# Hybrid decoder step: the first mixer group's next weights split ahead of its decay exponents, and the first head's attention steps at later places of the second group

## What is computed

```
proj = x @ w_in                               # 8 sections of 512: hq hf hv hg, rq rk rv rg
f    = lb + (1-lb)*sigmoid(hf);  log_f = log(max(f, 1e-6));  k = (1-lb)*sigmoid(-hf)
o_hg = HGRN2(silu(hq), k, hv, log_f)          # 4 heads of 128: decayed scores, running state
o_hg = rms_norm(o_hg) * g * silu(hg)
o_rt = retention(rotary(rq), rotary(rk), rv)  # 4 heads of 128
o_rt = (group_norm(o_rt)*g + b) * silu(rg)
x    = layer_norm(alpha*x + concat(o_hg, o_rt) @ w_o)
x    = layer_norm(alpha*x + conv_ffn(x))
```

## Time and profile before

| | |
|---|---|
| median of 3 timed runs | 1771.18 us |
| lowest and highest | 1766.13 and 1771.87 us |
| span of the profiled execution | 1765.4 us |
| own time of the profiled execution | not listed apart from its span |
| PE busy (matmul) | 1585.4 us, 90% of the span |
| DVE busy | 930.3 us, 53% |
| ACT busy | 657.9 us, 37% |
| POOL busy | 154.2 us, 9% |

### The profile page before, as it was taken

One profiled execution on the slowest core, in us unless ns is written; L12 is line 12 of the kernel. 1 busy time (PEld: TensorE's weight loads), 2 busy tenths in 40 slices (PEclk: granted clock), 3 DMA queues, 4 the chain that ended last, 5 costly groups with the idle time before them and its releaser, 6 DMA issues.

```text
span 1765.4 us, 31743 instructions
## 1 busy us (share of the span) xinstructions
PE 1585.4 (90%) x12187; PEld 1263.6 (72%) x12187; DVE 930.3 (53%) x1493; ACT 657.9 (37%) x936; POOL 154.2 (9%) x126
## 2 busy tenths in 40 slices
PE   4699999998879999999957999999896999999994
PEld 3577777776658888878745777777674888887883
DVE  5766744443575555533266767444366555553334
ACT  3635423232263433422154544233235443333223
POOL 3111110000020000000030111100002000000002
PEclk8789889998989999999978989999987999999997
DMA  5121231220312233223321222222121323322321
GB/s 185 51 62 51 73 109 62 84 73 26 96 50 94 95 95 95 73 79 90 97 66 48 73 73 73 76 85 73 50 74 47 96 95 95 95 80 71 98 65 51
DMA packets 175036, 137.86 MB, mean 78 GB/s; under 512 B 5064, under 2 KB 169192, under 8 KB 174776
## 3 DMA queue, kind: packets, MB, share of 16 engines
q1 hardware_dynamic: 168192, 113.46, 21.1%
q0 software_dynamic: 5408, 18.60, 3.1%
q10 hardware_dynamic: 1372, 4.95, 0.8%
HBM read 124.91 MB, written 12.07 MB: 78 GB/s over the span
## 4 chain that ended last, share of the span: by engine, by line
PE 76%; DVE 10%; ACT 6%; issue 4%; DVEq 3%; ACTq 1%; DMA 1%; SPq 0%
PE ACC L506 60%; PE SCR L619 2%; PE SCR L536 2%; PE OT L627 2%; ACT WH L825 1%; PE SCR L657 1%; DVE X L1189 1%; PE OT L679 1%; DVE Z L1220 1%; PE OT L595 1%; DVE Fb L1202 1%; DVE WL L1149 1%; DVEq L1259 1%; PE SCR L722 1%; PE OT L594 1%
## 5 line engine op out<-in xcount | busy, mean ns | idle before, releaser
L506 PE MATMUL ACC<-XH,WH 128*128 128x280 f16 x2432 | 503.7, 290 | 74.7 <-DVE XL L1192 43.1
L506 PE MATMUL ACC<-XL,WH 128*128 128x280 f16 x2432 | 502.6, 289 | 0.0
L506 PE MATMUL ACC<-XH,WL 128*128 128x280 f16 x2432 | 502.2, 289 | 0.0
L506 PEld LDWEIGHTS ACC<-XH,WH 128*128 128x128 f16 x2432 | 237.4, 101 | 158.7 <-DVE XL L1192 45.9
L1149 DVE SCALAR_TENSOR_TENSOR WL<-stage,WH 128x2048 f16<-128x2048 f32 (+1 forms) x116 | 245.9, 2120 | 180.8 <-ACT WH L825 169.1
L506 PEld LDWEIGHTS ACC<-XL,WH 128*128 128x128 f16 x2432 | 243.4, 100 | 58.8
L506 PEld LDWEIGHTS ACC<-XH,WL 128*128 128x128 f16 x2432 | 243.5, 100 | 58.4
L825 ACT ACTIVATE WH<-stage 128x2048 f16<-128x2048 f32 (+1 forms) x116 | 204.8, 1765 | 103.0 <-PE ACC L506 85.7
L506 PE MATMUL ACC<-shared,WH 128*128 128x280 f16 x1408 | 225.4, 283 | 0.2
L506 PEld LDWEIGHTS ACC<-shared,WH 128*128 128x128 f16 x1408 | 137.6, 98 | 30.7 <-issue 0.8
L506 PE MATMUL ACC<-shared,WL 128*128 128x280 f16 x704 | 141.3, 283 | 0.0
(11 more groups left out here) (241 smaller groups left out, 1870.7 us busy)
## 6 DMA issues: line engine op xcount, KB each, us to landing
stage<-in_w_in_dram SPq DMA_DIRECT2D x64, 512.0 KB, 4.8
stage<-in_w_a_dram SPq DMA_DIRECT2D x44, 512.0 KB, 4.2
stage<-in_w_b_dram SPq DMA_DIRECT2D x44, 512.0 KB, 4.6
stage<-in_w_down_dram SPq DMA_DIRECT2D x32, 384.0 KB, 3.1
stage<-in_w_down_dram SPq DMA_DIRECT2D x32, 320.0 KB, 3.4
out_dram<-shared POOLq DMA_DIRECT2D x16, 512.0 KB, 3.4
stage<-in_w_o_dram SPq DMA_DIRECT2D x16, 512.0 KB, 3.9
shared<-in_state_hgrn_dram POOLq DMA_DIRECT2D x8, 512.0 KB, 5.8
```

The costliest lines, as they stand in the source:

```text
L506: last = mm(ACC[:, acc, h, 0:HALF], lhs, x[:, xk + k, h * HALF:(h + 1) * HALF], start=begin, stop=end)
```

## The change

In group 0 of each layer, ACT writes the high part of the next unit of half 0 ahead of the read of q and of `hg_exponentials`, and DVE its low part ahead of `hg_exponents`; both stood behind them. Group 1 is taken out of the loop on PE and on DVE, and the loop now runs over groups 2 and 3. In group 1 DVE makes the low part of half 1 ahead of `hg_scores`, and PE places all attention steps of the first head by a new table: scores, transposes and state steps seven slots later, the sample steps, outputs and mean squares three slots later. No instruction is added to or taken from the computation.

```diff
@@ PE
                 group(l, 0)
-                with pe.Fori(0, HEADS - 1) as p:
+                group(l, 1, hg_steps(l, 0, scr_hg(l, 0), HG_SLOTS_FIRST))
+                with pe.Fori(1, HEADS - 1) as p:
                     group(l, p + 1, hg_steps(l, p, scr_hg(l, p), HG_SLOTS))
@@ ACT, group
                 if b is not None:
                     b()
+                if a is None:
+                    split_hi(0, j + 1, (acc_full, 1 + tile + 2))
                 if kind == 0:
                     if d is None:
                         read_acc(Q, 1, tile + 1, None)
                     hg_exponentials(l, head)
                     if d is not None:
                         read_acc(Q, 1, tile + 1, None)
-                split_hi(0, j + 1, (acc_full, 1 + tile + 2))
+                if a is not None:
+                    split_hi(0, j + 1, (acc_full, 1 + tile + 2))
                 if kind == 0:
                     hg_query(l, head)
@@ DVE, hg_query
-            def hg_query(l, p, j, mixed, steps):
+            def hg_query(l, p, j, mixed, steps, split_done=False):
...
-                split_lo(0, j)
+                if not split_done:
+                    split_lo(0, j)
@@ DVE, group
-            def group(l, g, head, kind, stages=(None,) * 4, mixed=None, after_hgrn=False):
+            def group(l, g, head, kind, stages=(None,) * 4, mixed=None, after_hgrn=False, split_first=False):
...
-                if a is not None:
+                if a is not None and not split_first:
                     a()
                 split_lo(1, j)
+                if split_first:
+                    a()
                 if kind == 0:
                     hg_gate(l, head, tile)
+                    if a is None:
+                        split_lo(0, j + 1)
                     hg_exponents(l, head)
...
-                    hg_query(l, head, j + 1, mixed, steps)
+                    hg_query(l, head, j + 1, mixed, steps, a is None)
@@ DVE, layer
                 group(l, 0, 0, 0)
-                with dve.Fori(0, HEADS - 1) as p:
+                group(l, 1, 1, 0, hg_stages(l, 0), ot0 + 2, split_first=True)
+                with dve.Fori(1, HEADS - 1) as p:
                     group(l, p + 1, p + 1, 0, hg_stages(l, p), ot0 + 2 + p)
@@ places
 HG_SLOTS = ([1, 2, 3, 4, 5, 6, 7], [7, 8, 9, 10], [12, 13], [22, 22], [23, 23, 24, 24, 25, 25], [28, 28])
+HG_SLOTS_FIRST = ([8, 9, 10, 11, 12, 13, 14], [14, 15, 16, 17], [19, 20], [25, 25], [26, 26, 27, 27, 28, 28], [31, 31])
```

## The result

The changed kernel takes 1784.39 us, the median of four runs (1781.68 to 1785.97). The kernel before, run beside it, takes 1770.2 us. The ratio is 1.0086, with a 95% interval from 1.0068 to 1.0104: slower, by 14 to 15 us, and outside the 0.3% that count as no change. The forecast was 1784.4 us. The profiled execution has a span of 1782.2 us, 16.8 us more than before (18.3 were forecast), and its own time is 1783.78 us.

What follows compares the result with a forecast made beforehand. PE bounds the kernel, through its waits and granted clock. Group 1's later ends (5.0 and 10.1 us) and group 2's start (3.2) add 18.3 to the 1765.4 us span; with 0.7 that gives 1784.4 us, 8-in-10 range 1772 to 1791.

Steps and rivals of the forecast that it cites:

- Weights ahead of the exponents: Group 0: low part ready at 70.7, tile 3 delayed by at most 1.8 us, QD at 84.7 as before.
- What ends PE's wait then: Start of group 1: PE waits for ACT's read of v, starting at 82.2; the wait shrinks by 2.83 us.
- Scores seven slots later: Group 1: first scores at 90.7, last transposes at 104.0, 2.4 us later in layer 0, 2.9 in layer 1.
- Sample steps at slot 25: Group 1, tile 3: PE waits 9.7 us at slot 24 for ACT's read of q, until 120.7 and 978.4.
- The rest of group 1: Behind the slot 24 wait: 20.4 us to the group's end, making it end 5.0 and 10.1 us later.
- the half-rate case: Rest of group 1 at half rate where the old 21.1 us tail had it: 20.4 us.
- The rival with a full-clock tail: Rest of group 1 takes 15.1 us, total +7.7 us, 1773.8 us; chance 0.14.
- Start of group 2: PE stands 1.6 us a layer ahead of group 2's third scores: +3.2 us for both layers.
- Code: Second copy of the group on PE and DVE: counted 0, at worst 3 instruction pieces a layer, 8.4 us.
- Sum: Whole kernel: 5.0 + 10.1 + 3.2 = +18.3 us on the 1765.4 us span, plus 0.7: 1784.4 us.
- The rival on the faster side: Group 1: accumulators ACC[0] and ACC[1] already free when PE comes, 1755 us; chance 0.06.

Runs made afterwards that it cites:

- Run 6: Changed kernel with ACT's read of v in group 0 moved ahead of the exponentials, q of group 1 still late: 1779.68 us, ratio 1.0062 to the kernel before.
- Run 1: Changed kernel with the first head's steps put back at the places of the other heads, early split kept: 1771.51 us, ratio 1.0004 to the kernel before.
- run 4: Changed kernel with ACT reading q ahead of the exponentials in all HGRN2 groups, places unchanged: 1765.85 us, ratio 0.9979 to the kernel before.
- run 5: Kernel before the change with one edit, q of all HGRN2 groups read ahead of the exponentials: 1770.49 us, ratio 0.9995 to the unedited kernel.
- run 7: Changed kernel with both v of group 0 and q of all HGRN2 groups read ahead of the exponentials, places unchanged: 1766.0 us, ratio 0.9983.
- run 10: Changed kernel with v and q read early, group 1 steps placed still later, sample steps of groups 2 and 3 at slot 26: 1753.15 us, ratio 0.9906.

## Why the prediction was right

**Weights ahead of the exponents.** Right: low part ready at 71.08 (70.7 forecast), QD started at 84.88 (84.7). The delay of tile 3 came to 0.95 us (up to 1.8), hidden in layer 0 and in layer 1 by the stop that follows.

**What ends PE's wait then.** Right in name and size: 82.44 behind ACT's read of v (82.2). Run 6 moves that read ahead and the wait goes with it, so this is shown.

**Scores seven slots later.** First scores at 90.76 (90.7), last transposes at 104.03 (104.0). Run 1 against the changed kernel shows that the new places, taken together, carry the loss, and run 4 that they do so only while q is read late.

**Sample steps at slot 25.** PE stood 9.77 us (9.7) and resumed at 120.82 (120.7); in layer 1 it resumed 37.93 us behind the restart (978.4 - 939.9 = 38.5). Shown by runs 4 and 5, which move nothing but the read.

**The rest of group 1.** 20.5 and 21.9 us (20.4 for both, so 1.5 too little in layer 1), the half-rate case. The rival with a full-clock tail, 15.1 us, fell in both layers. The rule cited from the Trainium skill, page "TensorE: Matmul & The Clock Gate", section "HAM oscillation", that the price of throttling is half of the throttled time, holds here too: the granted clock is a mean over the two levels 0.50 and 1.00, so that price is 20.5 x (1 - 0.64) = 7.4 us and 21.9 x (1 - 0.60) = 8.8 us, and both leave 13.1 us for the same work at full clock.

**Start of group 2.** The wait at the third scores came, 1.22 us a layer against 1.6: this term was a little too large.

**Code.** Nothing measurable: run 1 has the second copies and is level with the kernel before. The instruction queue moves 46 pieces instead of 41.

**Sum.** +16.8 on the span, +18.3 forecast. Group 1 cost no less than forecast: the first scores of group 2 come 5.2 us later in layer 0 (5.0), and in layer 1, counted from the first tile of the layer, 10.9 us later (10.1); the third scores add 2.4 (3.2). The other -1.8 us or so lie where no work was moved. In layer 0 slow and quick tails changed places (from group 2 to 3 the first scores are now 49.9 us apart instead of 43.8, and from there to group 4 43.8 instead of 48.4), which nearly cancels; in layer 1 the same groups take 1.2 us less. The stretch from group 4 of layer 0 to layer 1 is 3.0 us shorter than before, and the one from group 4 of layer 1 to the end is 2.1 us longer. No run takes these apart. The profiled execution's own time lies 1.6 us above its span, not 0.7, and the median 0.6 us above that. So the mechanism is shown, but that 1784.4 meets the median to the tenth is luck: 1.5 us too much in the sum and 0.9 + 0.6 us too little behind it.

The rival on the faster side had its mechanism right and its gain too large: with both accumulators free (run 7) the time is 1766.0 us, not 1755. In layer 0 of run 7 the scores start at 85.75 (85.4) and the sample steps 13.4 us behind the last transposes, as that sum had it. But the scores to transposes take 15.5 us instead of 13.26, at a clock of 0.84, and the rest of the group 15.8 us instead of 14.35, at 0.78.

## What to carry to other kernels

Before an input is made early, list everything that the waiting instruction needs, and look at where each of them stands in its engine's queue: the profile names only the last to come, and here the next one let PE start only 2.6 us sooner (82.44 for 85.03). A step that is moved to a later place is moved behind every wait between the two places, so look up each of those waits, above all for buffers that another engine frees in order behind unrelated work. Here the cheap move was the one that frees the buffer, one line on ACT; only with it did the later places pay, and then by 0.2% (run 4).

## What the runs showed of the hardware that was not expected

Behind its long waits PE ran at a lower clock, and there the loss was more than the length of the wait: the granted clock was 0.64 and 0.60 behind the 9.8 us stop of the changed kernel and 0.76 behind the 5.06 us wait of run 4. An early start that ends in a wait can give back part of its gain: run 7 started the scores 5.1 us earlier than run 4 and kept 2.8 us of it at the sample steps, since the stretch between ran at 0.84 instead of 1.00.

The tails behind waits of 2.8 us in front of the sample steps ran at either 0.90 (16.5 us) or 0.69 (21.1 us) in the kernel before, though groups 1 to 3 are one loop body there; which group gets which changes between kernels, and a difference of some 5 us between two of them need not come from the edit.

Nor does a lower clock need such a wait. In run 10 no wait stands ahead of the sample steps of groups 2 and 3. In group 2 of layer 0 the clock behind them was 1.00, but in group 2 of layer 1 it was 0.88, although PE was busy without a break from 978.60 to 1016.50, the first 23.4 us of it at 1.00. So run 10 does not show that the lost waits brought the clock back. What sets the clock in these stretches was not tried.
